# One weight split, two weight-set reads and the bias load put later in a two-layer retention and attention kernel

## The chip, the cores and the metric

The kernel runs on one NeuronCore of one Trainium2 chip. The metric is the device time of one execution in microseconds (us), the median of three runs. The engines are TensorE (PE in the rows; its weight loads are PEld), VectorE (DVE), ScalarE (ACT), GpSimd (POOL) and SyncE (SP), which here only issues transfers. GpSimd issues transfers too, on a queue of its own.

## The reference

A sequence of 2048 rows of width 1024 goes through two layers in fp32. Layer 0 is multi-scale retention, layer 1 is sliding-window attention with grouped keys and values, a bias table and sinks. Each ends in a post-LayerNorm.

```python
def retention_layer(x, w_in, w_out, pos):
    h = x @ w_in
    q, k, v, g = jnp.split(h, [D_MODEL, 2 * D_MODEL, 2 * D_MODEL + RET_WIDTH], axis=-1)
    ...
    def step(state, inp):                    # per chunk of 64 rows
        qn, kn, vn = inp
        cross = jnp.einsum('bhcd,bhde->bhce', qn, state) * xi
        state = state * g_chunk + jnp.einsum('bhcd,bhce->bhde', kn * zeta, vn)
        return state, cross
    ...
    r = inner + cross.transpose(1, 2, 0, 3, 4)
    r = (r - mu) * lax.rsqrt(var + GN_EPS)
    return (jax.nn.silu(g) * r) @ w_out

def swa_layer(x, w_in, w_out, sinks, k_band, v_band, bias, key_valid):
    q, gate = jnp.split(x @ w_in, 2, axis=-1)
    sc = jnp.einsum('bncvgd,bnkvd->bvgnck', q, k_band) + bias[None, :, :, None]
    ...
    return (o * jax.nn.silu(gate)) @ w_out

# x = post_norm(x, retention_layer(...)); k_band, v_band from kv = x @ swa_w_kv
# x = post_norm(x, swa_layer(...))
```

## The kernel before, in words

**Blocks and slots.** The sequence is cut into four blocks of 512 rows (`s` = 0 to 3). Each block walks through 134 slots, and in a slot TensorE works through one pair of weight tiles, 512 KB. Slots 0 to 71 are four retention heads of 18 slots: 4 for q and k, 14 for v and the gate g. Slots 72 to 99 (from `RO`) multiply by the retention layer's output weights, 100 to 103 (from `KV`) make the shared keys and values, 104 to 119 make q and gate of the attention layer, with the attention itself (`attend`) beside slots 108 and on, and 120 to 133 (from `SO`) multiply by the output weights.

**Weights.** fp32 products are made from three products of fp32r parts. So each pair is loaded by SP into a ring `stage` (`load_pair`, L538, four slots ahead), ScalarE rounds it to `w_hi` (`make_hi`, L1040) and VectorE writes the rest over it as `w_lo` (`make_lo`, L1403), both three slots ahead. TensorE waits for `w_lo` of its slot.

**Sums of weights.** The products by v, g and the output weights use a Strassen scheme with 7 instead of 8 products (P1 to P7). The sums of weight quarters that it needs are made once: 28 sets, which GpSimd's queue reads from memory (`load_t`, L2072, two transfers of 512 KB for each set), VectorE sums (`begin_t`, `end_t`, L1460 to L1467) and GpSimd's queue stores to `t_prep` (`store_t`, L2077). `T_PLAN` says for each set in which buffer, in which block and at which slots it is read, begun and ended. Sets 24 to 27 are done late in block 0 and sets 0 to 3 late in block 1. In a slot, GpSimd's program puts `store_t` ahead of `load_t`. At slots 96 and 100 it computes the reciprocal roots of the LayerNorm (`inverse_root`, L2102).

**A retention head.** Inside a head `v` counts the 14 slots of v and g. `retain(H, t)` for the four row tiles t are TensorE's retention steps; the first three stand in slots v = 7, 10 and 13 (in head 0 of blocks 0 and 1, which is `plain`, elsewhere). Behind step t VectorE does `after_retain(H, t)`: statistics (L1599), variance, the new state (L1588 or L1591), the next step's scores, `nmr` (L1477) and `st_lo` (L1558). ScalarE, at v = 8, makes `st_hi` (L1125), normalizes (L1129) and then, at v = 9, empties the two x banks of product P7 into `sg` (`empty`, L1045). TensorE's product P4, at v = 10, waits for those banks. In most slots VectorE's program begins with `make_lo`; `late_lo` names slots in which it doesn't, and there the program puts it elsewhere in the slot.

**Order at slot 100.** TensorE does all of the key and value products at once (`kv_block`, L820 and others). They wait for `w_hi` of slots 100 to 103, and in their course for the LayerNorm's last two tiles (L1728), which TensorE transposes (L780). Afterwards SP moves keys and values between partitions by five transfers (L656 to L659, at slot 106), for which the first scores of the attention wait (`score_pair`, L949, in slot 108). Between them SP stores sums of the next block's x (`x_sums`, L607 and L609), each when VectorE has split it (L1441), which it does behind the `make_lo` of its slot. The bias for the softmax, 8 transfers of 64 KB (L641), is needed in slot 108.

Of the kernel before, what the change touches and what calls it, by code (L numbers as in the profile page):

```python
# [65 lines left out]
VG = 4  # L66
RO, KV = 72, 100
# [42 lines left out]
def emptied(s, p, m):  # L110

    c = m // 2
    return 2 * (s * len(FILLS[c]) + FILLS[c].index(p)) + m % 2 + 1


def first_pair(kind, h, q):

    return PAIRS.index((kind, h, q, 0))
# [12 lines left out]
def vacant(g):  # L131

    return g // NP < PLAIN_BLOCKS and g % NP in VACANT
# [6 lines left out]
def ahead(g, n=AHEAD):  # L140

    return REAL[RING[g] + n] if g in RING and RING[g] + n < len(REAL) else NS * NP
# [12 lines left out]
def plain_head(H):  # L155

    return H % RH == 0 and H // RH < PLAIN_BLOCKS
# [13 lines left out]
def n_state(n):  # L171
# [13 lines left out]
T_BUF = {n: b for n, b, _, _, _, _ in T_PLAN}  # L185
T_RANK = {n: i + 1 for i, (n, _, _, _, _, _) in enumerate(T_PLAN)}
T_NTH = {n: [x[1] for x in T_PLAN[:T_RANK[n]]].count(b) for n, b, _, _, _, _ in T_PLAN}
# [14 lines left out]

def late_lo(H):

    return () if plain_head(H) else (VG + 3, VG + 11)


def retain_slots(H):
# [33 lines left out]
def build(nc, a):  # L242
    with ExitStack() as ctx:
# [205 lines left out]
        def bias_band(j, kvh):  # L449

            off = (4 * kvh + 2 * j) * REP + CHUNK - 1
            return bass.AP(bias_rep.tensor, off, [[NREL - 1, CHUNK], [REP, 2], [1, BAND]])
# [73 lines left out]
        def _(sp):  # L526
# [64 lines left out]
            for s in range(NS):  # L591
                for p in range(NP):
# [20 lines left out]
                    H = RH * s + h  # L613
# [17 lines left out]
                    if p in (RO + 14, RO + 19):  # L631
# [1 line left out]
                        sp.wait_ge(gated, 16 * (s + 1))  # L633
                        sp.dma_start(gb[:, i, :], a[("ln_gain", "ln_bias")[i]][0].partition_broadcast(P))\
                            .then_inc(gb_loaded, 16)
                    if p == KV:
                        if s == 0:
                            sp.wait_ge(bias_spread, 16)
                        for i in range(2):
                            for kvh in range(KVH):  # L640
                                sp.dma_start(bias[i * CHUNK:(i + 1) * CHUNK, 2 * kvh:2 * kvh + 2, :],  # L641
                                             bias_band(i, kvh)).then_inc(bias_loaded, 16)
# [741 lines left out]
        def _(dve):  # L1384
# [8 lines left out]
            def link(ins):  # L1393

                mark(ins)
                dve.wait_ge(dve_chain, chain[0])

            def make_lo(g):

                if g >= NS * NP or vacant(g):  # L1400
                    return
                dve.wait_ge(w_hi_made, SPLITS[g])
                nc.vector.tensor_tensor(w_lo[:, RING[g] % LS], stage[:, RING[g] % LS], w_hi[:, RING[g] % HS].bitcast(F32),  # L1403
                                        sub).then_inc(w_split, 1)
# [171 lines left out]
            def after_retain(H, t):  # L1576

                s, h = divmod(H, RH)
                n = 4 * H + t

                def new_state(d):
                    dve.wait_ge(dstate_full, 2 * n + d + 1)
                    if s == NS - 1 and t == NT - 1:
                        dve.sem_inc(state_ready, 1)
                    elif s == 0 and t == 0:
                        if h >= 2 and d == 0:
                            dve.wait_ge(state_stored[h % 2], 16)
                        nc.vector.tensor_copy(state[:, h % 2, d, :], bank[6 + d][:]).then_inc(state_ready, 1)  # L1588
                    else:
                        dve.wait_ge(state_ready, 2 * n + d - 1)  # L1590
                        nc.vector.scalar_tensor_tensor(  # L1591
                            out=state[:, h % 2, d, :], in0=state[:, h % 2, d, :], scalar=STATE_DECAY[h],
                            in1=bank[6 + d][:], op0=ALU.mult, op1=add).then_inc(state_ready, 1)

                early = h == RH - 1 and t == NT - 1
                if early:
                    new_state(0)
                dve.wait_ge(r_full, n + 1)
                link(nc.vector.bn_stats(stats[:, t, 0, :], bank[5][:]))  # L1599
                variance(t, stats[:, t, 0:1, :])  # L1600
                for d in range(int(early), 2):
                    new_state(d)
                if t + 1 < NT:
                    evacuate_score(H, t + 1)
                minus_mean(24 * s + 4 * h + t, t)
                if t + 1 < NT:
                    state_to_lo(H, t + 1)
# [240 lines left out]
            for s in range(NS):  # L1848
                for p in range(NP):
                    g = s * NP + p  # L1850
                    h, j = divmod(p, HEAD)
                    H = RH * s + h
# [23 lines left out]
                    if h < RH and j >= VG:  # L1876
# [35 lines left out]
                            after_retain(H, retain_slots(H).index(j - 1))  # L1912
                        if not plain_head(H) and v == 8:
                            after_retain(H, 0)
                        if not plain_head(H) and v == 10:
                            dve.wait_ge(x_free, emptied(s, first_pair("vg", h, "P7"), 1))
                            nc.vector.tensor_tensor(sg[:, 2:4, :], sg[:, 2:4, :], accs[:, 2:4, :], add)\
                                .then_inc(y_free, 2)
# [344 lines left out]
```

## Time and profile before

| | |
|---|---|
| time, median of 3 runs | 2338.75 us (2337.65 to 2338.89) |
| the profiled execution: its time, its span | 2340.16 us, 2337.9 us |
| TensorE busy | 2290.1 us (98%), 11554 matmuls |
| TensorE weight loads busy | 1901.4 us (81%) |
| VectorE busy | 1756.7 us (75%) |
| ScalarE busy | 1158.8 us (50%) |
| GpSimd busy | 345.9 us (15%) |
| moved by the DMA engines | 437.06 MB, mean 187 GB/s |
| mean granted TensorE clock | 0.994 of full speed |

Busy is the time in which an engine had an instruction running. The span is the time from the first to the last instruction of that one execution. The clock is a share of 2.4 GHz; 0.5 is its lower level, 1.2 GHz.

### The profile page before, as it was taken

Reading aid. Unit: us, or ns where it says so; the run is one execution under the profiler, and the core shown is the slowest. Engines: PE = TensorE matmul, PEld = TensorE weight load, DVE = VectorE, ACT = ScalarE, POOL = GpSimd, SP = SyncE. Lnnn points to the kernel's source line nnn. Section 1 sums busy time; section 2 is a strip of 40 time slices with the busy share of each in tenths; the row PEclk is TensorE's granted clock in tenths of the full one; section 3 lists DMA queues with packets and bytes.
Section 4 is the critical chain, followed back from the end, with each engine's and each line's share of the span. In section 5 each row is a group of like instructions: output and inputs, shape, how many; then the busy total and the mean of one; then the engine's idle time right before and its main releaser. Section 6 shows DMA issues by size and latency. Waiting matters only on the chain.

```text
span 2337.9 us, 30729 instructions
## 1 busy us (share of the span) xinstructions
PE 2290.1 (98%) x11554; PEld 1901.4 (81%) x11554; DVE 1756.7 (75%) x2439; ACT 1158.8 (50%) x1701; POOL 345.9 (15%) x346
## 2 busy tenths in 40 slices
PE   8999999999999999999999999999999999999997
PEld 6878877878888888887888888888888888888885
DVE  7888798875857669887596866897568667788548
ACT  4344455366435445636654544553655445554463
POOL 2311210222010110112201001110210110011132
PEclk9999999999999999999999999999999999999998
DMA  8787668653725435865484454585257345455323
GB/s 307 268 297 242 231 224 285 211 201 124 272 92 168 144 124 176 294 221 180 138 287 134 162 168 130 174 276 189 72 191 261 127 135 162 128 189 161 119 89 127
DMA packets 130899, 437.06 MB, mean 187 GB/s; under 512 B 13825, under 2 KB 18449, under 8 KB 130753
## 3 DMA queue, kind: packets, MB, share of 16 engines
q1 hardware_dynamic: 113088, 369.28, 47.7%
q0 software_dynamic: 17664, 65.83, 8.0%
q8 instruction: 92, 1.51, 0.3%
q14 instruction: 55, 0.44, 0.1%
HBM read 373.45 MB, written 57.41 MB: 184 GB/s over the span
## 4 chain that ended last, share of the span: by engine, by line
PE 83%; DVE 9%; DMA 4%; issue 3%; ACT 1%; SPq 0%; POOL 0%; DVEq 0%; ACTq 0%; POOLq 0%
PE accs L674 23%; PE accs L676 22%; PE accs L675 22%; PE bank L674 3%; PE bank L676 3%; PE bank L675 3%; DVE w_lo L1403 2%; PE bank L780 1%; PE bank L965 1%; PE bank L949 1%; PE bank L886 1%; PE bank L931 1%; DMA stage<-t_prep 1%; DMA stage<-w_qk 1%; PE accs L820 1%
## 5 line engine op out<-in xcount | busy, mean ns | idle before, releaser
L1403 DVE TENSOR_TENSOR w_lo<-stage,w_hi 128x1024 fp32r<-128x1024 f32 x524 | 643.8, 1236 | 330.0 <-ACT w_hi L1040 329.3
L1040 ACT ACTIVATE w_hi<-stage 128x1024 fp32r<-128x1024 f32 x524 | 550.3, 1055 | 482.6 <-PE accs L676 173.7
L674 PE MATMUL accs<-w_hi,xs 128*128 128x512 f32 x1136 | 450.5, 397 | 9.1 <-ACT sg L1045 6.4
L676 PE MATMUL accs<-w_hi,xs 128*128 128x512 f32 x1136 | 444.2, 391 | 0.0
L675 PE MATMUL accs<-w_lo,xs 128*128 128x512 f32 x1136 | 443.6, 390 | 0.0
L674 PEld LDWEIGHTS accs<-w_hi,xs 128*128 128x128 f32 x1136 | 213.9, 188 | 56.6 <-issue 12.1
L676 PEld LDWEIGHTS accs<-w_hi,xs 128*128 128x128 f32 x1136 | 213.8, 188 | 45.3
L675 PEld LDWEIGHTS accs<-w_lo,xs 128*128 128x128 f32 x1136 | 214.1, 188 | 42.3
L674 PE MATMUL accs<-x_hi,w_hi 128*128 128x512 f32 (+1 forms) x640 | 244.4, 382 | 1.9 <-DVE qT L1827 1.5
L2102 POOL TENSOR_TENSOR rstd<-ve,half 128x1 f32<-128x1 f32 x96 | 79.5, 829 | 1120.8 <-DVE ve L1473 880.3
L676 PE MATMUL accs<-x_hi,w_lo 128*128 128x512 f32 (+1 forms) x640 | 236.8, 370 | 0.0
L675 PE MATMUL accs<-x_lo,w_hi 128*128 128x512 f32 (+1 forms) x640 | 236.1, 369 | 0.0
L674 PE MATMUL accs<-xs,w_hi 128*128 128x512 f32 x512 | 204.0, 398 | 1.0 <-DVE w_lo L1403 1.0
L676 PE MATMUL accs<-xs,w_lo 128*128 128x512 f32 x512 | 201.0, 392 | 0.0
L675 PE MATMUL accs<-xs,w_hi 128*128 128x512 f32 x512 | 200.7, 392 | 0.0
L674 PE MATMUL accs<-w_hi,ra 128*128 128x512 f32 x448 | 177.3, 396 | 0.5 <-DVE ra L1447 0.5
L676 PE MATMUL accs<-w_hi,ra 128*128 128x512 f32 x448 | 175.5, 392 | 0.0
L675 PE MATMUL accs<-w_lo,ra 128*128 128x512 f32 x448 | 175.3, 391 | 0.0
L674 PEld LDWEIGHTS accs<-x_hi,w_hi 128*128 128x128 f32 x640 | 120.8, 189 | 28.0 <-issue 8.0
L676 PEld LDWEIGHTS accs<-x_hi,w_lo 128*128 128x128 f32 x640 | 120.8, 189 | 21.0
L675 PEld LDWEIGHTS accs<-x_lo,w_hi 128*128 128x128 f32 x640 | 121.1, 189 | 17.4
L1125 ACT ACTIVATE st_hi<-state 128x1024 fp32r<-128x1024 f32 x60 | 63.5, 1059 | 132.9 <-DVE state L1591 117.1
(207 smaller groups left out, 3780.8 us busy)
## 6 DMA issues: line engine op xcount, KB each, us to landing
stage<-t_prep SPq DMA_DIRECT2D x208, 512.0 KB, 3.7
stage<-w_vg SPq DMA_DIRECT2D x100, 512.0 KB, 3.5
stage<-w_qk SPq DMA_DIRECT2D x64, 512.0 KB, 3.5
stage<-w_swa SPq DMA_DIRECT2D x64, 512.0 KB, 3.9
t_prep<-t_buf POOLq DMA_DIRECT2D x28, 1024.0 KB, 5.7
stage<-w_ro SPq DMA_DIRECT2D x48, 512.0 KB, 3.5
cs<-rope_t SPq DMA_DIRECT2D x16, 1024.0 KB, 7.8
t_buf<-w_vg POOLq DMA_DIRECT2D x32, 512.0 KB, 9.4
```

The lines of the kernel that those rows point to most:

```text
L674: mm(dst, lhs[0], rhs[0], start=start, stop=False, skip_group_check=reopened)
L675: mm(dst, lhs[0], rhs[1], start=False, stop=False, skip_group_check=reopened)
L676: return mm(dst, lhs[1], rhs[0], start=False, stop=stop, skip_group_check=reopened)
L780: tr = nc.tensor.transpose(dst[:, e * P:(e + 1) * P], src[:, e * P:(e + 1) * P], ident[:])
L820: nc.tensor.matmul(acc[2 + t][:, 0:KVC], x, w, start=start, stop=stop)
L886: mm = nc.tensor.matmul(bank[4][:, 2 * P:3 * P], krT[:, d, ts], qrT[:, d, ts], start=d == 0, stop=d == 1)
L931: tr = nc.tensor.transpose(bank[5][:, i * P:(i + 1) * P], pr[:, u // 2 % 3, u % 2, i, 0:BAND], ident[:])
L949: mm = nc.tensor.matmul(bank[4 + 3 * e][:, at_:at_ + BAND], qT[rows, c, 2 * kvh:2 * kvh + 2, :].rearrange("p a q -> p (a q)"), kT[rows, kv ...
L1040: copy(w_hi[:, RING[g] % HS], stage[:, RING[g] % LS], ACT.Copy).then_inc(w_hi_made, 1)
L1125: copy(st_hi[:], state[:, h % 2], ACT.Copy).then_inc(state_hi_made, 1)
L1403: nc.vector.tensor_tensor(w_lo[:, RING[g] % LS], stage[:, RING[g] % LS], w_hi[:, RING[g] % HS].bitcast(F32), sub).then_inc(w_split, 1)
L2102: tt(rstd[:, i:i + 1], ve[:, i:i + 1], half[:], ALU.pow).then_inc(rstd_ready, 1)
```

## The change

`late_lo` gets the slot v = 8 of each head that isn't plain (14 of 16), and `make_lo` of that slot goes behind `after_retain(H, 0)`. The reading of sets 25 and 26 (block 0) and 1 and 2 (block 1) goes from slot 100 to slot 102. The bias load goes from slot 100 to slot 103, in all four blocks.

```diff
@@ T_PLAN: set, buffer, block, slot of reading, of begin, of end
-          (24, 0, 0, 88, 100, 100), (25, 2, 0, 100, 108, 108), (26, 3, 0, 100, 110, 110), (27, 4, 0, 103, 112, 112),
-          (0, 0, 1, 88, 100, 100), (1, 2, 1, 100, 108, 108), (2, 3, 1, 100, 110, 110), (3, 4, 1, 103, 112, 112)]
+          (24, 0, 0, 88, 100, 100), (25, 2, 0, 102, 108, 108), (26, 3, 0, 102, 110, 110), (27, 4, 0, 103, 112, 112),
+          (0, 0, 1, 88, 100, 100), (1, 2, 1, 102, 108, 108), (2, 3, 1, 102, 110, 110), (3, 4, 1, 103, 112, 112)]
@@ late_lo
-    return () if plain_head(H) else (VG + 3, VG + 11)
+    return () if plain_head(H) else (VG + 3, VG + 8, VG + 11)
@@ SP's program
-                    if p == KV:
+                    if p == KV + 3:
                         if s == 0:
                             sp.wait_ge(bias_spread, 16)
                         for i in range(2):
@@ VectorE's program
                         if not plain_head(H) and v == 8:
                             after_retain(H, 0)
+                            make_lo(ahead(g))
```

TensorE's and ScalarE's orders are the same. On VectorE, the first head that isn't plain is head 1 of block 0, and around its slot v = 8 the order before was:

```order
L1573 TENSOR_TENSOR att_lo<-att,att_hi 128x128
L1403 TENSOR_TENSOR w_lo<-stage,w_hi 128x1024 x3
L1599 BN_STATS stats<-bank 128x6
...
L1477 SCALAR_TENSOR_TENSOR nmr<-mv,rstd 128x1
L1558 TENSOR_TENSOR st_lo<-state,st_hi 128x1024
L1403 TENSOR_TENSOR w_lo<-stage,w_hi 128x1024
L1460 TENSOR_TENSOR t_buf_90<-t_buf_90 128x512
```

and is now:

```order
L1573 TENSOR_TENSOR att_lo<-att,att_hi 128x128
L1403 TENSOR_TENSOR w_lo<-stage,w_hi 128x1024 x2
L1599 BN_STATS stats<-bank 128x6
...
L1477 SCALAR_TENSOR_TENSOR nmr<-mv,rstd 128x1
L1558 TENSOR_TENSOR st_lo<-state,st_hi 128x1024
L1403 TENSOR_TENSOR w_lo<-stage,w_hi 128x1024 x2
L1460 TENSOR_TENSOR t_buf_90<-t_buf_90 128x512
```

One `w_lo`, that for slot v = 11, moved from ahead of the thirteen instructions behind the retention step to behind them.

On GpSimd's queue around slots 96 to 103 of block 0 (`t_buf_88` holds set 24, `_90` set 25, `_91` set 26, `_92` set 27) the order before was:

```order
L2089 DMA part_74<-x_turned 128x4x256
L2102 TENSOR_TENSOR rstd<-ve,half 128x1 x2
L2072 DMA t_buf_90<-w_so 128x2x512 x2
L2072 DMA t_buf_91<-w_so 128x2x512 x2
L2102 TENSOR_TENSOR rstd<-ve,half 128x1 x2
L2077 DMA t_prep<-t_buf_88 128x4x512
L2072 DMA t_buf_92<-w_so 128x2x512 x2
```

and is now:

```order
L2090 DMA part_74<-x_turned 128x4x256
L2103 TENSOR_TENSOR rstd<-ve,half 128x1 x4
L2078 DMA t_prep<-t_buf_88 128x4x512
L2073 DMA t_buf_90<-w_so 128x2x512 x2
L2073 DMA t_buf_91<-w_so 128x2x512 x2
L2073 DMA t_buf_92<-w_so 128x2x512 x2
```

The four reads of sets 25 and 26 moved behind two reciprocal roots and behind the store of set 24, which waits until VectorE has summed that set, so that six reads now follow one another.

On SP, from slot 100 of block 0 on, this piece of the difference shows where the bias went:

```order
 L538 DMA stage<-w_kv 128x1024 x4
-L538 DMA stage<-w_swa 128x1024
+L538 DMA stage<-w_swa 128x1024 x4
 L641 DMA bias<-bias_rep 64x2x128 x8
-L538 DMA stage<-w_swa 128x1024 x5
+L538 DMA stage<-w_swa 128x1024 x2
 L607 DMA x_sums<-sum_hi_102 128x1024
 L609 DMA x_sums<-part_lo_78 128x1024
```

The eight bias transfers moved behind the weight loads for slots 105, 106 and 107, and stand right ahead of those for 108 and 109.

## Rows read from the trace of the kernel before

**Rows 1.** The page: TensorE busy, share of the span.

```profile
PE 2290.1 (98%) x11554; PEld 1901.4 (81%) x11554; DVE 1756.7 (75%) x2439; ACT 1158.8 (50%) x1701; POOL 345.9 (15%) x346
```

**Rows 2.** Waits of TensorE: for whom; us in total, times, longest.

```profile
PE accs L674 <- ACT sg L1045: 6.4, 3, 4.0
PE accs L820 <- ACT w_hi L1040: 5.2, 2, 2.8
```

**Rows 3.** Timeline, head 1 of block 0: start, us, what; idle before in brackets.

```profile
145.40 1.23 DVE L1403 TENSOR_TENSOR w_lo<-stage,w_hi 128x1024 fp32r<-128x1024 f32 x1 [2.99 <-ACT w_hi L1040]
147.33 1.23 DVE L1403 TENSOR_TENSOR w_lo<-stage,w_hi 128x1024 fp32r<-128x1024 f32 x1 [0.70 <-ACT w_hi L1040]
148.47 0.69 DVE L1599 BATCH_NORM_STATS2 stats<-bank 128x6 f32<-128x512 f32 x1
152.08 1.22 DVE L1558 TENSOR_TENSOR st_lo<-state,st_hi 128x1024 fp32r<-128x1024 f32 x1
153.60 0.47 PE L674 MATMUL accs<-w_hi,xs 128*128 128x512 f32 x1 [4.05 <-ACT sg L1045]
```

**Rows 4.** Timeline, head 3 of block 0 and slot 75.

```profile
306.40 1.22 DVE L1403 TENSOR_TENSOR w_lo<-stage,w_hi 128x1024 fp32r<-128x1024 f32 x1 [0.37 <-ACT w_hi L1040]
350.93 0.63 PE L780 MATMUL bank<-ident,r_out 128*128 128x128 f32 x4 [1.90 <-DVE state L1591]
```

**Rows 5.** Stretches: length, busy of the engines, granted clock, DMA share, GB/s.

```profile
154.50:158.00 3.50, 3.50 (x10) 2.70 (x9) 3.01 (x4) 1.33 (x2) 0.00 (x0) 0.51 0.50 199
359.00:362.50 3.50, 3.46 (x9) 2.78 (x10) 3.48 (x4) 2.16 (x3) 0.00 (x0) 0.55 0.55 221
427.50:431.00 3.50, 3.50 (x19) 3.50 (x18) 3.43 (x11) 0.00 (x0) 0.10 (x1) 0.52 1.14 220
1007.80:1011.30 3.50, 3.50 (x17) 3.32 (x16) 3.50 (x8) 0.62 (x2) 0.00 (x0) 0.51 1.09 296
```

**Rows 6.** Timeline (GpSimd's queue) and chain that ended last, slot 100 of block 0.

```profile
417.85 2.90 POOL L2072 DMA_DIRECT2D t_buf<-w_so  x4
...
418.09 6.87 DMA stage<-w_kv
```

**Rows 7.** Stretches from slot 100's start to the attention's first scores, blocks 2, 0, 1.

```profile
1577.40:1629.60 52.20, 51.50 (x327) 45.80 (x325) 38.40 (x49) 18.84 (x24) 3.07 (x2) 1.00 0.52 167
421.50:477.50 56.00, 52.86 (x325) 47.36 (x323) 41.54 (x53) 17.70 (x22) 5.28 (x5) 0.97 0.69 221
1003.40:1058.70 55.30, 52.69 (x325) 47.33 (x323) 41.12 (x53) 17.58 (x22) 5.29 (x5) 0.97 0.65 215
```

**Rows 8.** Timeline, the LayerNorm's last tile and TensorE's transposes, block 0.

```profile
435.55 1.28 DVE L1728 SCALAR_TENSOR_TENSOR z<-z,rstd,gb 128x1024 f32<-128x1024 f32 x1
438.72 1.91 PE L780 MATMUL bank<-ident,z 128*128 128x128 f32 x16
```

**Rows 9.** The chain that ended last, slots 103 to 108 of block 0.

```profile
452.53 8.83 DMA stage<-w_swa
...
470.93 6.55 DMA vs<-vcar
477.52 1.19 PE bank L949 x16
```

**Rows 10.** Timeline of ScalarE: the rounding of the weights for slot 106, block 0.

```profile
454.79 1.06 ACT L1040 ACTIVATE w_hi<-stage 128x1024 fp32r<-128x1024 f32 x1 [0.33 <-DMA stage<-w_swa]
```

**Rows 11.** Timeline, block 1, and the last copy's transfer: KB, us to landing.

```profile
1053.84 0.81 SPq L659 DMA_DIRECT2D vs<-vcar  x1
1058.73 1.16 PE L949 MATMUL bank<-kT,qT 64*128 64x128 f32 x16
...
vs<-vcar SPq DMA_DIRECT2D x1, 64.0 KB, 4.0
```

**Rows 12.** Stretches of block 0 behind slot 102, columns as in Rows 5.

```profile
454.00:463.00 9.00, 9.00 (x42) 7.46 (x41) 5.34 (x5) 5.15 (x6) 0.00 (x0) 1.00 0.96 386
463.00:478.00 15.00, 14.90 (x72) 12.10 (x72) 7.86 (x8) 5.60 (x7) 0.00 (x0) 1.00 1.03 321
```

## The prediction

> **What bounds the kernel now.** First the page, for the share of TensorE: 98% of the span [rows 1]. A change that only moves instructions can win back idle TensorE time and time at the lower clock, and nothing else. So next the waits of TensorE, for where that idle time lies: two entries lead, 6.4 us in three waits for the emptying of P7's banks (`sg`, L1045) and 5.2 us in two waits for `w_hi` in the key and value block (L820) [rows 2]. These are also the two places that the change touches. Then the granted clock by stretch: it is full but for four short stretches, in which it is near a half [rows 5]. They follow idle time: the first comes behind the 4.05 us at v = 10 of head 1 [rows 3], the last two behind the waits of L820, of which the longer is 2.8 us and so the shorter 2.4 us [rows 2]. The second, at 359 us, is in the region of the waits for VectorE's last state of head 3 [rows 4]. A stretch of 3.5 us at 0.51 loses 3.5 x 0.49 = 1.7 us. Idle times of 1.1 to 1.2 us at the other two waits for `sg` (6.4 - 4.05 = 2.35 for both) had none behind them. I therefore charge 1.7 us for a single idle time of 2.36 us or more, and nothing for a shorter one.
>
> **The order on VectorE, head 1 of block 0.** Before, VectorE finishes slot v = 7's `w_lo` at 145.40 + 1.23 = 146.63, waits 0.70 us for v = 8's `w_hi`, splits it, and starts on `after_retain` at 148.47 [rows 3]. ScalarE needs what comes out of that (state, then `nmr`) before it gets to `sg`, for which TensorE stands idle 4.05 us. With the split behind, `after_retain` starts at 146.63, 1.8 us earlier, and so does everything up to TensorE's restart. 2.2 us of idle time remain, a little under the shortest idle time that had a slow stretch behind it, so that I count the slow stretch as gone too: -1.8 and -1.7. **Head 2**: only the split's own 1.1 us (147.33 to 148.47 in [rows 3]) is saved, nearly all of that wait: -1.1. **Head 3**: its wait of some 1.1 us goes as well, but from there VectorE has its own backlog up to the state for which TensorE waits 1.90 us at 350.93 [rows 4]; who comes earlier there waits longer. What VectorE itself gains is the 0.37 us for which it waited at 306.40 [rows 4]: -0.4. The other eleven heads have no wait of TensorE for `sg` [rows 2], so nothing comes of it there.
>
> What it costs: the moved `w_lo` is for slot v = 11. It now comes 152.08 + 1.22 - 148.47 = 4.8 us later in relation to its old place [rows 3]. Between TensorE's restart and that slot lie one more pair and the second retention step, 27 matmuls, and VectorE is finished with it before TensorE even restarts. I take 0. If that cover were gone, the most it could cost is the same 4.8 us in a head.
>
> **Reads of sets 25 and 26 (and 1 and 2).** Before, their four transfers go out from 417.85 on, at the moment of the last key and value weights (418.09), which then land after 6.87 us [rows 6], while TensorE waits in L820. Of the same stage there is a clean copy: block 2, which has no such sets, needs 52.2 us from slot 100 to the first scores, blocks 0 and 1 need 56.0 and 55.3 with clock 0.97 [rows 7]. The change takes the reads out of this place. What is then late next is the LayerNorm: its last tile is ready at 435.55 + 1.28 = 436.83, and TensorE transposed it in the second half of L780, from 438.72 + 0.96 = 439.68 on [rows 8]. TensorE can come at most 2.9 us earlier, so of the 3.8 us between blocks 0 and 2 I take 2.9. In block 1 the difference is 3.1 and the wait in front was 0.45 shorter; I take 2.6. This holds the two slow stretches as well. Sum -5.5 us.
>
> **Where the reads and the bias go.** GpSimd now issues them behind set 24's store, at about 451 us, where SP's queue is busiest, and SP's bias load stands right ahead of the weights for slot 108. Here is a chain with no room in block 0: those weights land at 452.53 + 8.83 = 461.36, ScalarE and VectorE split them and then the second sum of x, which SP stores, and behind that store come the five copies of keys and values. The last is issued at 470.93, lands 6.55 us later at 477.48, and TensorE takes up the scores at 477.52 [rows 9], with practically no wait. Whatever makes the weights of slot 108 later makes TensorE wait by as much.
> How much: with GpSimd's queue busy too, SP's queue landed the weights of slot 106 at 454.79 [rows 10] and those of 108, two loads on, at 461.36 [rows 9], so 3.3 us for 512 KB. The bias is 8 x 64 KB = 512 KB. Hence +3.3 us in block 0. In block 1 the last copy lands at 1053.84 + 4.0 = 1057.8 and the scores start at 1058.73 [rows 11]: 0.9 us of room, +2.4 us. Both are at or over 2.36 us, so two new slow stretches: +3.4. Blocks 2 and 3 have the bias move but no reads. In 52.2 us block 2 has a DMA share of 0.52 against 0.69 in block 0 [rows 7], and I take 0.
> The bounds. No cost at all, if the 16 engines carry the surplus beside what they do: behind 463 us they moved 321 GB/s, where 386 were reached with both queues busy [rows 12]. At most: 4 x 512 KB + 512 KB = 2.62 MB pass the 386 GB/s one after the other before the last copy, 6.8 us in block 0 and 5.9 in block 1. I take the middle, which the landing times give.
> The Trainium skill ("DMA: Bandwidth & Descriptors", section "Issuing engines are not separate DMA queues") says that transfers issued by different engines all run on the same 16 DMA engines and interleave, so another queue saves issue time only. This speaks for the upper bound. The same page gives about 436 GB/s as the ceiling ("Where 436 GB/s comes from"); by that figure the bound would be 6.0 us rather than 6.8, an estimate. No row here reaches it.
>
> **Sum.** -1.8 - 1.7 - 1.1 - 0.4 - 5.5 + 3.3 + 2.4 + 3.4 = -1.4 us. The profiled execution took 2340.16 us, 1.4 above the median; it would come to 2338.8, and the median to 2338.75 - 1.4 = 2337.3 us.
>
> **The rivals.**
> - *The copies stay on time.* Everything above but the last three terms: -10.5 us, 2328.2. For it: throughput was higher with both queues busy [rows 12], and all copies shift with TensorE. Against it: no room in block 0 [rows 9], and 2.62 MB more in the way.
> - *Slower: one queue's worth of transfers in front of the copies.* Place: slot 108 of blocks 0 and 1. Price: 6.8 + 5.9 us of waiting and 3.4 us of slow clock, with -10.5: +5.6 us, 2344.3. It comes out slower than before as soon as the two waits together pass 10.5 - 3.4 = 7.1 us. For it: the four reads held up the key and value weights in just this way [rows 6]. Against it: the 3.3 us for a load is already measured beside a busy GpSimd queue.
> - *The order on VectorE wins nothing.* If TensorE meets another wait in the heads (the split now behind, or the LayerNorm and state work that VectorE does without pause), the 5.0 us of the heads go: 2342.3. Against it: VectorE found its inputs ready at L1599 in the rows, so it loses no filler work.
>
> **How the numbers follow.** About 0.2% (4.7 us) is what a measurement of this kernel tells from no change. Forecast 0.47; copies on time 0.33; copies far too late 0.14; heads win nothing 0.06. Faster by over 0.2% (under 2334.1) is the first rival and the low edge of the forecast: 0.35. Slower (over 2343.4) is the second and the high edge of the third: 0.15. The rest, 0.50, is the same. The range goes from 2327.5 to 2344.5, so that it reaches both rivals' values and leaves out their outer halves. The forecast's own range is 2334 to 2341.
>
> **What would show it.** Right, if the wait of L674 for `sg` falls from 6.4 to about 2.2 us with one entry left, the waits of L820 for `w_hi` are gone, a new wait of L949 for the copies (L656 to L659) stands in blocks 0 and 1 with 2 to 4 us each, and the granted clock dips behind that wait and no longer at 154, 427 and 1008 us. It is wrong if L949 doesn't wait, if the reads at 451 us land without delaying slot 108's weights, or if block 2 loses time at slot 108 because of the bias alone.

## The result, and the profile after

The changed kernel takes 2346.95 us (median of 6 runs, 2344.90 to 2350.01) where the kernel before, beside it, took 2337.61 us (2333.38 to 2338.89). The ratio is 1.0046, 95% interval 1.0033 to 1.0058: slower by 9.3 us by the medians and by 10.8 us by the ratio, where 1.4 us less had been predicted, and outside the range of 2327.5 to 2344.5 us. The profiled execution took 2349.67 us, with a span of 2347.4 us.

The page of the profile says what it said before [rows 1]: TensorE is busy for 98% of a longer span.

```profile
PE 2294.5 (98%) x11554; PEld 1900.4 (81%) x11554; DVE 1751.2 (75%) x2439; ACT 1158.9 (49%) x1701; POOL 346.1 (15%) x346
```

The waits of TensorE (for whom; us in total, times, longest) show both intended gains, and the new waits beside them:

```profile
PE accs L674 <- ACT qT L1045: 5.1, 2, 2.7
PE bank L949 <- DMA vs<-vcar: 4.4, 2, 2.4
...
PE accs L674 <- ACT sg L1045: 1.8, 1, 1.8
...
PE accs L820 <- DVE w_lo L1403: 1.5, 3, 0.6
...
PE accs L820 <- ACT w_hi L1040: 0.3, 1, 0.3
```

The wait for `sg` fell from 6.4 us in three to 1.8 us in one, that of L820 for `w_hi` from 5.2 to 0.3 us [rows 2]. Two entries are new: the first product of slot 108 waits for the emptied `qT` banks, and the first scores wait for the copies, once in each of blocks 0 and 1, together 9.5 us.

The stretches (length, busy of the engines, granted clock, DMA share, GB/s) add the clock. These four lie behind those four waits. Two more are in the heads, near 280 and 358 us, as many as before; the stretches behind head 1, and at slot 100 in blocks 0 and 1, [rows 5] are gone. The end of the execution is slow too, from 2334 us on, and loses 7 to 9 us in every kernel here. The prediction's "full but for four short stretches" left this out, and it makes no difference between the kernels.

```profile
474.30:477.80 3.50, 3.50 (x10) 2.41 (x8) 3.29 (x4) 1.47 (x2) 0.00 (x0) 0.51 0.99 266
481.10:484.60 3.50, 3.50 (x11) 2.76 (x9) 3.27 (x6) 1.78 (x2) 0.00 (x0) 0.51 1.02 412
1061.40:1064.90 3.50, 2.96 (x8) 1.80 (x6) 2.83 (x3) 1.06 (x1) 0.00 (x0) 0.51 1.00 255
1068.20:1071.70 3.50, 3.50 (x10) 2.72 (x9) 3.46 (x5) 2.45 (x3) 0.00 (x0) 0.51 1.03 420
```

**Where the copies lose their time.** Two stretches of block 0, the key and value block and from there to the first scores, of the kernel before:

```profile
425.00:447.00 22.00, 20.81 (x158) 20.38 (x159) 18.27 (x28) 4.08 (x7) 3.07 (x2) 0.92 0.33 88
447.00:480.00 33.00, 32.75 (x176) 27.59 (x176) 21.16 (x24) 15.07 (x17) 2.20 (x3) 1.00 0.92 314
```

and of the changed kernel:

```profile
425.00:447.00 22.00, 20.88 (x174) 20.44 (x173) 21.47 (x33) 3.24 (x5) 3.29 (x3) 1.00 0.07 22
447.00:480.00 33.00, 28.27 (x124) 22.57 (x122) 16.26 (x17) 12.43 (x14) 4.81 (x7) 0.95 0.98 326
```

Before, part of the late reads and the bias fell into the 22 us in which the DMA engines are otherwise nearly idle (share 0.33, now 0.07). The change put them into the 33 us behind, where the share was 0.92 already. The chain that ended last in that stretch (start, us, what; SPq is SP issuing, L641 is the bias, L607 and L609 store a sum of x, L656 to L659 are the copies):

```profile
447.60 0.62 SPq L641
...
454.43 0.61 SPq L641
455.08 12.69 DMA stage<-w_swa
467.79 1.07 ACT w_hi L1040
...
471.27 0.32 SPq L607
471.63 0.43 SPq L609
...
476.32 3.62 DMA vs<-vcar
479.99 1.16 PE bank L949 x16
```

Two things make the load for slot 108 late. SP needs 7.4 us to issue the eight transfers of the bias (447.60 to 455.04), and the load is issued only behind them. Then it takes 12.69 us to land, against 8.83 before [rows 9]. ScalarE waits for it (start, us, what, idle time before in brackets):

```profile
467.79 1.06 ACT L1040 ACTIVATE w_hi<-stage 128x1024 fp32r<-128x1024 f32 x1 [11.43 <-DMA stage<-w_swa]
...
471.60 1.06 ACT L1066 ACTIVATE sum_hi<-part 128x1024 fp32r<-128x1024 f32 x1 [0.85 <-DMA x_sums<-part_lo]
472.68 1.09 ACT L1045 ACTIVATE qT<-accs 128x512 f32<-128x512 f32 x2
```

Behind it come the sums of x, one of which waits until the store before has landed, and only then the `qT` banks are emptied, which is the first of the two new waits. VectorE's and SP's work for the copies hangs on the same load: the second.

Blocks 2 and 3, where only the bias moved, lose little or nothing: block 2 takes 52.35 us from the transposes of slot 100 to the first scores (1586.11 to 1638.46), and took 52.2 before [rows 7]; block 3 takes 52.0 (2150.33 to 2202.34), and took 51.3.

### The profile page after: what moved, and what is told of

It reads as the page before. It is cut to its first block, busy times and chain, and to the rows that moved or that the text cites. A ratio compares the mean times of both kernels' runs of the same rounds, so it can differ in the third digit from the quotient of the medians.

```text
span 2347.4 us, 30729 instructions
## 1 busy us (share of the span) xinstructions
PE 2294.5 (98%) x11554; PEld 1900.4 (81%) x11554; DVE 1751.2 (75%) x2439; ACT 1158.9 (49%) x1701; POOL 346.1 (15%) x346
## 4 chain that ended last, share of the span: by engine, by line
PE 78%; DVE 11%; DMA 5%; issue 4%; SPq 1%; ACT 1%; POOL 0%; DVEq 0%; ACTq 0%; POOLq 0%
PE accs L674 22%; PE accs L676 21%; PE accs L675 21%; DVE w_lo L1403 3%; PE bank L674 2%; PE bank L676 2%; PE bank L675 2%; PE bank L949 1%; PE bank L965 1%; DMA stage<-t_prep 1%; PE bank L780 1%; PE bank L931 1%; DMA stage<-w_swa 1%; DVE z L1728 1%; PE bank L886 1%
## 5 line engine op out<-in xcount | busy, mean ns | idle before, releaser
L674 PE MATMUL accs<-w_hi,xs 128*128 128x512 f32 x1136 | 449.7, 396 | 6.7 <-DVE krT L1495 2.1
L674 PEld LDWEIGHTS accs<-w_hi,xs 128*128 128x128 f32 x1136 | 213.9, 188 | 53.8 <-issue 5.9
L674 PE MATMUL accs<-x_hi,w_hi 128*128 128x512 f32 (+1 forms) x640 | 246.7, 385 | 5.8 <-ACT qT L1045 5.1
L674 PE MATMUL accs<-xs,w_hi 128*128 128x512 f32 x512 | 203.9, 398 | 1.3 <-DVE w_lo L1403 0.9
L674 PE MATMUL accs<-w_hi,ra 128*128 128x512 f32 x448 | 177.4, 396 | 0.6 <-DVE ra L1447 0.5
L674 PEld LDWEIGHTS accs<-x_hi,w_hi 128*128 128x128 f32 x640 | 121.9, 191 | 32.7 <-issue 9.3
L1190 ACT ACTIVATE pr<-pr,lowest 128x129 f32<-128x129 f32 x256 | 99.7, 393 | 51.6 <-DVE lowest L1814 51.6
```

What stands on the lines that cost most here:

```text
L674: mm(dst, lhs[0], rhs[0], start=start, stop=False, skip_group_check=reopened)
L1190: exped = copy(scores, scores, ACT.Exp, bias=lowest[:, n:n + 1], scale=-1.0, accum_out=rsum[:, n:n + 1])
```

## The experiments

Each ratio is to the kernel before, run beside (medians 2334.74 to 2337.61 us), so the ratios compare better than the times. "Waits" are the two entries L674 for `qT` and L949 for the copies together, in both blocks; "slow" is the time lost to the lower clock behind them, read from stretches of 0.5 us. Both are of one profiled execution. In kernels with fewer lines ahead of it, L949 is L946 or L942. The rows "heads" have VectorE's new order, "all" is the whole change.

| kernel | ratio to before, 95% | waits, us | slow, us |
|---|---|---|---|
| heads only | 0.9986 [0.9976, 0.9995] | 0 | 0 |
| heads, reads at slot 94 | 0.9983 [0.9973, 0.9992] | 0 | 0 |
| heads, one of two reads at 102 | 0.9990 [0.9980, 1.0001] | 1.3 | 0 |
| heads, bias at 103 | 0.9994 [0.9985, 1.0003] | 3.3 | 0 |
| heads, reads at 94, bias at 103 | 0.9995 [0.9986, 1.0004] | 3.1 | 0 |
| heads, reads at 102 and 107 | 1.0006 [0.9997, 1.0016] | 7.5 | 3.4 |
| heads, reads at 102 | 1.0014 [1.0004, 1.0024] | 6.7 | 5.1 |
| bias at 103 only | 1.0016 [1.0007, 1.0026] | 3.3 | 1.7 |
| reads at 102 only | 1.0032 [1.0020, 1.0044] | 6.7 | 5.1 |
| all, bias as one transfer | 1.0027 [1.0015, 1.0038] | 9.1 | 6.8 |
| all, bias at 104 | 1.0033 [1.0021, 1.0046] | 10.6 | 5.1 |
| all, bias on GpSimd's queue | 1.0035 [1.0021, 1.0049] | 10.9 | 5.1 |
| all, again | 1.0038 [1.0024, 1.0051] | 10.7 | 6.8 |
| all | 1.0046 [1.0033, 1.0058] | 9.5 | 6.8 |

### One part at a time

Heads only:

```diff
-    return () if plain_head(H) else (VG + 3, VG + 11)
+    return () if plain_head(H) else (VG + 3, VG + 8, VG + 11)
...
+                            make_lo(ahead(g))
```

> Only the order on VectorE in the heads is changed; reads and bias stand as before. Theory A (the heads win what the trace after shows and lose most of it again before slot 100): 0.5 to 3 us less than before, L674's wait for sg down to one of about 2 us in head 1. Theory B (the heads' terms of the forecast hold to the end): 5 us less. Theory C (the order in the heads is what made the changed kernel slower): 5 to 9 us more.

2332.09 us, ratio 0.9986: this part alone wins 3.2 us (1.2 to 5.6), between the values of theories A and B and not apart from either. Theory C has fallen. Reads only:

```diff
-          (24, 0, 0, 88, 100, 100), (25, 2, 0, 100, 108, 108), (26, 3, 0, 100, 110, 110), (27, 4, 0, 103, 112, 112),
+          (24, 0, 0, 88, 100, 100), (25, 2, 0, 102, 108, 108), (26, 3, 0, 102, 110, 110), (27, 4, 0, 103, 112, 112),
...
```

> Only the reads of sets 25, 26 and 1, 2 go to slot 102. Theory A (SP's queue advances one piece for each piece of GpSimd's queue, so without the bias ahead the weights of slot 108 lose little): the waits of L820 for w_hi go (6 us less), the copies are up to 2 us late in each block: 2 to 6 us less than before in all. Theory B (bytes alone count: 2.1 MB more ahead of the copies at 386 GB/s): 5.4 us of waiting in each of two blocks and two slow stretches, 6 to 9 us more than before.

2343.03 us, ratio 1.0032: 7.5 us slower with no bias in the way, as theory B had it, though with 3.2 and 3.5 us of waits for the copies and not 5.4 each. Its waits and ScalarE's timeline show another link of the chain than in the whole change: not the weights of slot 108, for which ScalarE waits 1.13 us, but the store of a sum.

```profile
PE bank L949 <- DMA vs<-vcar: 6.7, 2, 3.5
```

```profile
458.89 1.06 ACT L1040 ACTIVATE w_hi<-stage 128x1024 fp32r<-128x1024 f32 x1 [1.13 <-DMA stage<-w_swa]
...
470.01 1.06 ACT L1066 ACTIVATE sum_hi<-part 128x1024 fp32r<-128x1024 f32 x1 [5.92 <-DMA x_sums<-part_lo]
```

Bias only:

```diff
-                    if p == KV:
+                    if p == KV + 3:
```

> Only the bias load goes to slot 103. Theory A (the 512-byte pieces of the bias each wait for a 4 KB piece of GpSimd's queue, which has set 24's store and set 27's read there): the weights of slot 108 some 4 to 5 us late in blocks 0 and 1, the copies with them, and slow stretches: 8 to 12 us more than before. Theory B (bytes alone: 512 KB at 386 GB/s): 1.4 us in each block, 1 to 3 us more in all, no slow stretch.

2338.82 us, ratio 1.0016, +3.7 us (1.6 to 6.1), with 3.3 us of waits for the copies and one slow stretch. It is far from theory A. Theory B's range overlaps, but it had no slow stretch. Heads and reads together, the bias left at slot 100:

> The change without its bias part. Theory A (the bias in the middle of the reads is what costs): the long landing of slot 108's weights goes, 3 to 8 us less than before. Theory B (the reads themselves cost): 3 us or more above before, near the changed kernel.

2338.06 us, ratio 1.0014: 6.5 us over the heads alone, with the same 6.7 us of waits as with the reads only. So the largest part of the loss is the reads', and theory A, in which the bias in the middle of them is what costs, has fallen. Heads and bias together:

> The whole change but the later reads: VectorE's order in the heads and the bias at slot 103, with sets 25, 26 and 1, 2 read at slot 100 as before. If the parts add: -3.2 us of the heads and +3.7 of the bias alone, so 1.0002 of before (+0.5 us, 0.9990 to 1.0014). If the reads and the bias need each other for the loss (the whole lost more than its parts): under 0.9995. If the heads' gain is worth nothing once slot 108 is late: 1.0012 to 1.0020.

2334.28 us, ratio 0.9994 [0.9985, 1.0003]: the parts add within the intervals (0.9986 times 1.0016 is 1.0002). The value lies in both of the first two ranges, so it doesn't decide between them. The three parts together give 0.9986 x 1.0032 x 1.0016 = 1.0034, inside the intervals of both measurements of the whole change (1.0046 and, again, 1.0038, with the same two waits in each of blocks 0 and 1).

### Bytes, pieces or places

The whole change with the eight transfers of the bias in one, of the same 512 KB. This kernel leaves the bias out: it loads other weights in its place, for the time alone.

```diff
-                        for i in range(2):
-                            for kvh in range(KVH):
-                                sp.dma_start(bias[i * CHUNK:(i + 1) * CHUNK, 2 * kvh:2 * kvh + 2, :],
-                                             bias_band(i, kvh)).then_inc(bias_loaded, 16)
+                        sp.dma_start(bias[:].rearrange("p (u a) n -> p u (a n)", u=2), w_kv[0]).then_inc(bias_loaded, 16)
...
-                dve.wait_ge(bias_loaded, 128 * (s + 1))
+                dve.wait_ge(bias_loaded, 16 * (s + 1))
```

> The whole change, but the bias load of slot 103 is one transfer of 512 KB in pieces of 4 KB (it reads the first key and value weights in place of the bias, so the bias in the scores is not the right one); before, it was eight transfers of 64 KB in pieces of 512 B. Theory P (pieces): SP's and GpSimd's queues alternate piece by piece, so small pieces beside GpSimd's 4 KB ones take the bytes' time eightfold. Then the load lands within some 3 us instead of 12.5 us for the eight, the weights of slot 108 are no longer late (ScalarE waits under 6 us for them instead of 11.4), the waits in front of the first scores of block 0 fall from 2.44 + 1.98 us to what the reads alone leave (3.1 us in one), and the time is 3 to 8 us below that of the whole change (1.0046 of before): 1.0014 to 1.0033. Theory B (bytes): only the number of bytes in front of the copies counts, the time stays at 1.004 to 1.006 of before, and slot 108's weights land as late as with the eight.

2342.81 us, ratio 1.0027, in the range of the theory of pieces. ScalarE's wait for the weights of slot 108, 11.43 us with eight transfers, is 3.27 us with one:

```profile
457.82 1.06 ACT L1037 ACTIVATE w_hi<-stage 128x1024 fp32r<-128x1024 f32 x1 [3.27 <-DMA stage<-w_swa]
...
466.72 1.06 ACT L1063 ACTIVATE sum_hi<-part 128x1024 fp32r<-128x1024 f32 x1 [5.20 <-DMA x_sums<-part_lo]
```

The reason that the theory gave isn't shown, though. The one transfer itself took 9.2 us to land and not 3. What changed most is the time in which SP issues: 0.44 us for the one against 7.4 us for the eight, so that the load for slot 108 goes out at 447.08 and not at 455.08 (start, us, what):

```profile
446.01 0.44 SPq L639 DMA_DIRECT2D bias<-w_kv  x1
```

```profile
447.08 10.72 DMA stage<-w_swa
```

This execution is 1.6 us ahead of the other by then (its L820 waits at 424.91, the other's at 426.49). So 6.4 us of the gain are issue time, and 2.0 us are the landing, 10.72 against 12.69.

But TensorE's wait only moved, to the store of the sum behind, and TensorE waits nearly as long as with the whole change, in one piece for each block:

```profile
PE bank L946 <- DMA vs<-vcar: 9.1, 2, 4.6
```

The ratio's interval overlaps with that of the whole change, so what was gained, if anything, is unclear. The same by way of place, with the bias one slot later, behind the weights of slot 108 on SP's queue (`p == KV + 4`):

> The whole change with the bias one slot later (104), so behind the weights of slot 108 on SP's queue and ahead of those of slot 109. Theory W (the bias costs because it makes the weights of slot 108 late, and through them ScalarE's work in front of the copies): the wait of ScalarE for those weights falls from 11.4 to some 5 us, the first of the two waits of block 0 at the start of the scores (L674, 2.44 us, and 2.41 in block 1 with the wait behind it) goes, and 1.0010 to 1.0032 of before, like the heads with the reads alone or with the bias as one transfer. Rival V (whatever stands in front of the second store of x's sums and the copies costs the same): that store and the copies land as late as with the whole change, and 1.0040 to 1.0055.

1.0033, between the two ranges and not apart from the whole change. Its profile decides against theory W, in which the late weights of slot 108 are the cause:

```profile
453.06 1.06 ACT L1040 ACTIVATE w_hi<-stage 128x1024 fp32r<-128x1024 f32 x1 [0.95 <-DMA stage<-w_swa]
466.09 1.06 ACT L1040 ACTIVATE w_hi<-stage 128x1024 fp32r<-128x1024 f32 x1 [11.02 <-DMA stage<-w_swa]
468.66 1.06 ACT L1066 ACTIVATE sum_hi<-part 128x1024 fp32r<-128x1024 f32 x1 [1.51 <-DMA x_sums<-part_lo]
```

The weights of slot 108 are there at 453 us. Those of slot 109 come 13 us later, and the emptying of `qT` behind them. The last copy doesn't wait for them: it is issued at 462.46 already and takes 14.44 us to land.

```profile
462.46 14.44 DMA vs<-vcar
```

The waits are 6.6 us for `qT` and 4.0 us for the copies. Last, the bias on GpSimd's queue, behind its reads:

```diff
+                    if p == KV + 4:
+                        pool.wait_ge(products, used(s * NP + KV - 1))
...
+                                pool.dma_start(bias[i * CHUNK:(i + 1) * CHUNK, 2 * kvh:2 * kvh + 2, :],
+                                               bias_band(i, kvh)).then_inc(bias_loaded, 16)
```

> The whole change, but the eight bias transfers are issued by GpSimd behind the reads of its queue, not by SP. The same bytes in the same stage. Theory T (the queues take turns, so what counts is what stands on SP's own queue ahead of the sums and the copies): the weights of slot 108 land as in the heads with the reads alone, one wait per block at the start of the scores, 1.0004 to 1.0028 of before. Theory B (all bytes in the stage count alike): 1.0030 to 1.0058, as the whole change. There is a third way, that the bias now lands too late for the first scores and VectorE waits for it, with a wait of TensorE in slots 109 to 111: over 1.005.

2343.18 us, ratio 1.0035: by its value and its waits theory B, though the interval reaches into the other range. On SP's queue the bias no longer stands in the way. The last copy is issued at 461.43, 15 us earlier than with the whole change (476.32), of which 4 us are this execution's being ahead (its L820 waits at 422.33). It takes 13.80 us to land:

```profile
461.43 13.80 DMA vs<-vcar
475.27 2.08 PE bank L942 x16
```

```profile
PE bank L942 <- DMA vs<-vcar: 10.9, 2, 5.7
```

So the same bytes in the same stretch cost about the same here, on whichever queue they stand and whoever issues them: what SP no longer spends on issuing, the copies wait for in landing. The Trainium skill ("DMA: Bandwidth & Descriptors", section "Issuing engines are not separate DMA queues") says that transfers of different engines run on the same 16 DMA engines and interleave. This run agrees, with 10.9 us of waits against 9.5 and 10.7.

### How much room there was

Heads, with set 26 (and 2) alone read at slot 102, 25 (and 1) left at slot 100:

> VectorE's order in the heads as changed, the bias at slot 100 as before, and of the two late sets only the second (26, and 2 in the next block) read at slot 102; 25 and 1 stay at slot 100. Half of the bytes move. Theory Q (bytes in front of the copies): half of the loss that both reads gave over the heads alone (+6.5 us of 0.9986 to 1.0014), so 0.9998 to 1.0004 of before, with a wait of L949 of some 1.5 us in each of blocks 0 and 1 in place of 3.2 and 3.6. Rival (any read behind the store of set 24 makes them late, since what is late is one transfer): 1.001 to 1.002. Other rival (there was room for half): as the heads alone, 0.9980 to 0.9995.

0.9990, and 1.3 us of waits for the copies, 0.7 us at most in one block. The value is that of the second rival, that there was room for half; its interval reaches into theory Q's range, but theory Q's waits of 1.5 us aren't there. Half of the bytes cost next to nothing, the other half 5.4 us of waits and the slow clock: there is room for about 1 MB in each block, and not for 2. The straight line from nothing to all was wrong. Heads, with set 25 at slot 102 and 26 held back until TensorE is done with slot 106:

```diff
+                if at_slot == 107:
+                    pool.wait_ge(products, used(in_block * NP + at_slot - 1))
```

> VectorE's order in the heads as changed, the bias at slot 100, set 25 (and 1) read at slot 102, and set 26 (and 2) held back until TensorE is done with slot 106, which is behind the issue of the copies; it is needed at slot 110. Theory Q (bytes queued ahead of the copies, with room for half of them): the same bytes in the same stage, but 1 MB fewer in front of the copies, so no wait of L949 over 0.8 us and 0.9980 to 0.9995 of before, like the half move. Rival (what counts is the load on the DMA engines in the whole stretch of slots 102 to 110): L949 or slot 110's weights wait 2 us or more, and 1.000 to 1.002.

1.0006 with 7.5 us of waits. The ratio lies in the rival's range, and its wait too. The last copy is issued at 460.79, the held-back read at 461.82, and still TensorE's wait for that copy ends only at 473.58 (start, us, what):

```profile
460.79 12.75 DMA vs<-vcar
473.58 1.16 PE bank L949 x16
```

so being issued behind the copies is not the same as being served behind them.

Heads, with the reads at slot 94, where the DMA engines have time:

> VectorE's order in the heads as changed, the bias at slot 100 as before, and sets 25, 26 and 1, 2 read at slot 94 in place of 100 or 102. Theory Q (bytes of GpSimd's reads ahead of the copies): it is the 3 MB in GpSimd's queue from 447 us on that made the store of x's sums and the copies late when the reads stood at slot 102 (+6.5 us against the heads alone). With the reads landed before set 24 is stored, the copies are issued and land at or before their time in the kernel before: no wait of the first scores (L949) over 0.5 us, no wait in the key and value block for weights, and 0.9970 to 0.9990 of before, so 0 to 4 us under the heads alone. Rival: the reads at slot 94 hold up the key and value weights or the second residual block's transfers instead, with a new wait in slots 94 to 100: 0.999 to 1.002.

2332.30 us, ratio 0.9983, and no wait of L949. It is not distinguishable from the heads alone. The rival's wait is there as well, but small: L820 waits 2.5 us for `w_hi` in four pieces, where theory Q had none. The same with the bias at 103:

> VectorE's order in the heads and the bias at slot 103 as changed, the two late sets read at slot 94. Theory I (the bias load costs only beside the reads): with sets 25, 26 and 1, 2 landed before the bias is issued, the eight pieces land one per 0.4 us, the weights of slot 108 are on time, no wait of L949 over 0.6 us, and the time is that of the same kernel with the bias at slot 100: 0.9983 of before (0.9973 to 0.9992). Theory S (512 KB in front of slot 108's weights cost by themselves what they cost over the heads alone with the reads at slot 100, 0.9986 to 0.9994): a wait of L949 of 1 to 2 us in blocks 0 and 1, and 0.9990 to 0.9996.

0.9995 and 3.1 us of waits, as much as with the reads at 100. The bias costs something by itself; theory I has fallen. Whether it is the 512 KB or the 7.65 us that SP takes here to issue them is open: no run has the bias alone in one transfer.

### Was there a wait in the key and value block?

The kernel before, profiled twice more:

> The kernel before once more, for a second profile. Theory C (the two waits of 2.8 and 2.4 us in the key and value block are chance: they occur when GpSimd's first late read and SP's last load of those weights are issued within 0.3 us, the read first): in two more profiles at least one of the four places has a wait of L820 for w_hi under 1 us. Theory D (they belong to the order of the kernel before): all four have over 2 us.

> The kernel before a third time, for a third profile. As for the second: Theory C wants a wait of L820 under 1 us in at least one of the four places of the two, Theory D over 2 us in all four.

Times 2334.83 and 2338.87 us. In the first, the order of issue at slot 100 of block 0, and the wait of L820 behind it:

```profile
414.15 0.33 SPq L538 DMA_DIRECT2D stage<-w_kv  x1
...
414.81 0.74 POOL L2072 DMA_DIRECT2D t_buf<-w_so  x1
...
423.89 1.46 PE L820 MATMUL accs<-w_lo,x_hi 128*128 128x256 f32 x10 [0.60 <-DVE w_lo L1403]
```

and in the second, in block 1:

```profile
997.63 0.75 POOL L2072 DMA_DIRECT2D t_buf<-w_vg  x1
...
997.75 0.33 SPq L538 DMA_DIRECT2D stage<-w_kv  x1
...
1005.28 2.56 PE L820 MATMUL accs<-w_hi,x_hi 128*128 128x256 f32 x10 [2.18 <-ACT w_hi L1040]
```

Three of the four places have some 0.6 us, one has 2.18 us. The last is the one in which the first read went out 0.12 us ahead of the last key and value load; in the other three it went out 0.65 us or more behind it. In the first profile it was 0.24 us ahead in block 0 [rows 6]. Theory C holds: the wait is there in some executions, decided by tenths of a microsecond. The profiles of "heads only", "bias at 103 only" and "heads, bias at 103", which also read at slot 100, bear it out. Of all twelve places, the read went out first in four, by 0.01 to 0.31 us, and these four have waits of 1.87 to 2.81 us and a slow stretch each. In the other eight it went out at least 0.07 us behind, and the waits are 0.36 to 0.96 us, with no slow stretch. "One of two reads at 102" fits too: in block 1 its read at slot 100 went out 0.01 us ahead, with a wait of 2.49 us and a slow stretch. In the eight kernels' profiles with the reads at slot 102 all sixteen places have 0.22 to 0.64 us and none a slow stretch.

## Why the prediction was wrong, step by step

**The heads (-1.8 - 1.7 - 1.1 - 0.4 = -5.0 us): right in kind, perhaps too large.** Alone they bring -3.2 us, with an interval from -5.6 to -1.2 that still holds the -5.0. The mechanism is as described: in head 1 VectorE now starts `after_retain` at once, and `w_lo` stands behind `st_lo`.

```profile
146.08 0.69 DVE L1599 BATCH_NORM_STATS2 stats<-bank 128x6 f32<-128x512 f32 x1
149.67 1.22 DVE L1558 TENSOR_TENSOR st_lo<-state,st_hi 128x1024 fp32r<-128x1024 f32 x1
150.81 1.22 DVE L1403 TENSOR_TENSOR w_lo<-stage,w_hi 128x1024 fp32r<-128x1024 f32 x1
```

```profile
151.20 0.47 PE L674 MATMUL accs<-w_hi,xs 128*128 128x512 f32 x1 [1.79 <-ACT sg L1045]
```

TensorE's idle time there is 1.79 instead of 4.05 us [rows 3]. What isn't reliable is the -1.7 for the slow stretch, nor the rule behind it (charge it from 2.36 us of idle time on, nothing below). The second profile of the changed kernel has 1.94 us there and a slow stretch behind it, and the kernel before has 2.78 us of idle time there in one of its other profiles and no slow stretch, and 4.31 us with one of twice the length in the other.

```profile
153.00 0.47 PE L674 MATMUL accs<-w_hi,xs 128*128 128x512 f32 x1 [2.78 <-ACT sg L1045]
```

```profile
153.63 0.77 PE L674 MATMUL accs<-w_hi,xs 128*128 128x512 f32 x1 [4.31 <-ACT sg L1045]
```

**The key and value block (-5.5 us): a real gain, priced at more than twice its mean.** The two waits and the slow stretches behind them were read from one execution and taken for a property of the order. They are there in three of the six places of the kernel before's three profiles. Over the six profiles with the reads at slot 100, the waits of L820 and the slow clock behind them come to 3.5 us for an execution, over the eight with the reads at 102 to 1.1 us. An estimate of what the later reads win is therefore -2.4 us. No run measures it alone, since later reads also make the copies late.

**The copies (+3.3 + 2.4 us, and +3.4 for two slow stretches): this step failed.** It was right in place and too small, because the sum charged the wrong bytes. "So 3.3 us for 512 KB" priced the bias and left out the four reads, which the upper bound had counted. The reason for leaving them out, "already measured beside a busy GpSimd queue", held for the 2 MB that stood on that queue before (set 24's store and set 27's read) and not for 4 MB. The sum also put nothing for SP's 7.4 us of issuing. Measured, the waits are 3.3 us for the bias and 6.7 us for the reads over both blocks, 9.1 to 10.9 for both, instead of 5.7. The upper bound, 6.8 + 5.9, held. Its reason did too: the rival "one queue's worth of transfers in front of copies" had the mechanism. Two waits for each block, for `qT` and for the copies, or one long one, brought 6.8 us of slow clock instead of 3.4. What comes back is small: two waits for VectorE's `qT` (L1827), 1.5 us in total with the heads alone, are gone in the changed kernel.

The sum by these terms: -3.2 (heads) - 2.4 (key and value block) + 9.5 (waits) + 6.8 (clock) - 1.5 = +9.2 us, beside the measured +9.3 us (+8 to +14 by the interval of 1.0046; +8.9 by the ratio 1.0038 of the second measurement). That it meets the number so closely is luck: of the other kernels with the reads at slot 102, the same sum with their own waits and slow clock comes out 0.6 to 2.5 us over the measured difference. That is about what their intervals allow, but all on one side, and whether part of the waits doesn't count stays open.

**The blocks 2 and 3 (0):** right for block 2 and within 0.7 us for block 3, as shown above.

**The prediction's tests:** L674 for `sg` at 2.2 us with one entry (1.8), the waits of L820 for `w_hi` gone (0.3), waits of L949 in blocks 0 and 1 of 2 to 4 us each (2.0 and 2.4, with 2.4 and 2.7 for `qT` ahead), no slow stretch at 154, 427 and 1008: all came true in this profile (the second one has a slow stretch at 152 us again), and the time still came out 10 us from the forecast. They tested whether each mechanism is there, and none asked what else is in front of the first scores.

## What to carry to other kernels

Before moving a transfer to a later slot, read the DMA share of the stretch that it leaves and of the one that it enters: here 0.33 and 0.92, and 2.6 MB went the wrong way. Read also how long the issuing engine is busy with it. Count all bytes that are served ahead of the first transfer which the critical engine waits for, on every queue, and take off the room that there is (1 MB cost next to nothing, the second 5.4 us of waits). Take a second profile of the kernel before ahead of pricing a wait of 2 us that depends on which of two queues issues first. The version to keep is VectorE's order alone, with the reads at slot 100 or 94 and the bias at slot 100 (0.9986 and 0.9983).

## What the runs showed of the hardware

- **Eight small transfers hold up the queue that issues them.** SP takes 5.17 us to issue the eight bias transfers of 64 KB in block 2, 7.4 and 8.0 us in blocks 0 and 1, where the DMA engines are busier, and 0.44 us for the same 512 KB in one transfer. That is most of the difference between ScalarE's waits of 11.43 and 3.27 us for the next load. The rest is some 2 us of landing. The profile's issues section has the bias's eight at 9.8 us each to landing in the window 421 to 470 us, and 6.4 us each in the kernel with the reads at slot 94, where GpSimd's queue was short. The Trainium skill ("DMA: Bandwidth & Descriptors", section "Queues, rings and completion order") says that each DMA engine goes round between its queues and takes a whole packet from one before it switches. Such turns could make pieces of 512 B slower beside larger ones; no run here shows a turn, or separates this from the load as a whole.
- **A small transfer can take four times as long to land.** The last copy, 64 KB, took 3.62 us to land with the whole change, and 12.75, 13.80 and 14.44 us in the three kernels that issue it earlier, at 460.79, 461.43 and 462.46. The copy had landed earlier by 6.4 us at most, though issued 14 to 16 us earlier.
- **The slow clock comes in equal portions.** In all profiles a place before the end of the execution has 0, 1.7 or 3.4 us of loss. After the single wait of 4.53 us, the kernel with the bias in one transfer had

```profile
476.50:483.30 6.80, 6.69 (x27) 5.48 (x28) 4.42 (x7) 3.84 (x10) 0.00 (x0) 0.51 0.87 357
```

so one long wait cost 3.4 us, as much clock as two short ones. Which it will be is not decided by the wait's length alone: 2.78 us had nothing behind it in the kernel before, 1.98 us had 1.7 us of loss behind it at the first scores of the changed one, where another wait and slow stretch lay just ahead.
